# The second slab of six feed-forward networks, computed from 512-column products of high and low activations

## The chip, the cores and the metric

The kernel runs on one core of a Trainium2 chip. The metric is the device time in microseconds (us) of one execution, the median of several. The kernel before takes 1621.5 us (three runs, 1621.46 to 1623.59).

## What is computed

The reference runs a sequence of 256 tokens, 1024 wide, in float32 through four mixers (HGRN2, sparse attention, stick-breaking attention with a convolution, gated linear attention) and six feed-forward networks. Networks 0 and 1 have a causal convolution of width 3 on the up-projection; networks 2 to 5 have none. With `D_FF` = 2816:

```python
def conv_ffn(x, w_up, conv_w, conv_b, w_down):          # networks 0 and 1
    h = x @ w_up
    C = h.shape[-1]
    h = lax.conv_general_dilated(h, conv_w[:, None, :].astype(h.dtype), window_strides=(1,),
                                 padding=[(CONV_WIDTH - 1, 0)],
                                 dimension_numbers=('NWC', 'WIO', 'NWC'),
                                 feature_group_count=C) + conv_b
    gate, up = jnp.split(h, 2, axis=-1)
    return (jax.nn.silu(gate) * up) @ w_down

def swiglu(x, w_in, w_out):                              # networks 2 to 5
    a, b = jnp.split(x @ w_in, 2, axis=-1)
    return (jax.nn.silu(a) * b) @ w_out
```

## The kernel before

**Numbers in two parts.** Every weight and every activation is held as a high part and a low part (the value less its high part), and a product is high times high, plus high times low, plus low times high. ScalarE makes the high part of a slab of weights (`high`, line 596), VectorE the low part (`low`, line 1361, or `low_one`, line 1283).

**Slabs.** A feed-forward network has NF = 11 slabs of 256 hidden columns, numbered from 0. Slab i needs three pieces of weights of 1 MB each: its gate columns (ring slot `c_`), its up columns (slot `d`) and its rows of the down-projection (slot `a`). SyncE loads them in a fixed order, each when its slot is free. Slab 0 alone is computed with the tokens as rows and turned afterwards (`turn_tokens`); slab 10 has code of its own.

**TensorE's order in a network** is written out by hand in `ffn`: the products of slab 0, `up_one` (gate and up of slab 1), `down(0, True)`, `up_sums(2, True)`, `down(1)`, then a loop of `up_sums(j + 3)` and `down(j + 2)`, and the last slab. Into `up_one` the four transposes of `turn_tokens(1)` are put, which end slab 0. So the gate and up of a slab are computed one step ahead of its down-projection.

**Two forms of gate and up.** `up_one` (slab 1) uses `features`: for each of 4 blocks of 128 hidden columns and each of 8 chunks of the contraction it makes three 256-column matmuls (`three`, lines 1935 to 1937). The gate lies in half a bank of PSUM and the up in the other half, banks 6 and 7. `up_sums` (slabs 2 to 9, in networks 2 to 5 also slab 10) uses `high_sums` (line 2111: one 512-column matmul for each chunk, the high weights against high and low activations side by side) and `low_sums` (line 2118: one 256-column matmul for each chunk). There a bank holds two halves that must still be added: VectorE does it in `sum_parts` (line 1388), one for each of the 4 blocks, gate in banks 4 and 5, up in banks 6 and 7.

**The down-projection** `down` makes 24 matmuls of 512 columns: 12 for the first token block (`tb` = 0, banks 0 and 1), then 12 for the second (`tb` = 1, banks 2 and 3). It waits for the low part of `a` and for the gated activations (`g_hi` by ScalarE at line 784, `g_lo` by VectorE at line 1374).

**VectorE's and ScalarE's orders** are written by hand too, and each engine goes through its own strictly. After slab 0 (`body(0, ...)`, with lines 1447, 1368 and 1374) VectorE does, for a slab in the form of sums, `body_of_sums`:

```python
sum_parts(i, 0, 0)
sum_parts(i, 0, 1)
low(c_, i + c0)
if conv:
    later_taps(i, 0, range(2))
sum_parts(i, 1, 0)
sum_parts(i, 1, 1)
```

and then the taps of the up, the gating, the low parts of `d`, of the gated values and of `a`. ScalarE's `body_of_sums` does `gates(i)` (the first taps at line 757 in networks 0 and 1, the Silu at line 766 in the others), then `high(c_)`, `ups(i)`, `high(d)`, the two `split` (line 784) and `high(a)`. The `low(c_)` and `high(c_)` of slab i are for the weights of slab i + 1.

Of the kernel before, what the change touches and what calls it, by code (L numbers as in the profile page):

```python
# [26 lines left out]
P = 128  # L27
# [40 lines left out]
CROSS_BANK = {HG_HEADS: 4, GLA_HEADS: 5}  # L68
WIDE = 2 * SLAB
HALF_K = NK // 2  # L70
HGRN_PAIRS = ((0, 1), (2, 3), (0, 1), (2, 3))
# [69 lines left out]
def build(nc, A, out):  # L141
    with ExitStack() as ctx:
# [223 lines left out]
        def sums_before(f):  # L366
            return f * (NF - 2) - min(f, 2)

# [216 lines left out]
        def _(act):  # L585
# [124 lines left out]
            def ffn(conv, f_conv, f):  # L710

                a, b_, c_, d = FFN_SLOTS[f]
                q0, h0, s0, t0 = f * NF, f * (NF - 1), sums_before(f), f_conv * (NF - 3)

# [18 lines left out]

                def start_gate(b, i, odd):
                    up_done(b, i)
                    i = 0 if i is None else i
                    bank = ps[:, 4 + 2 * odd + b, :]
                    if conv:
                        for g in range(2):
                            c = i * 2 + (row_of["ffn_conv_w"] + f_conv * 132 + 88 + g * 22 + b)  # L740
                            cb = i * 2 + (row_of["ffn_conv_b"] + f_conv * 44 + g * 22 + b)
                            ins = act.activation(ff_c[:, b, g, :], bank[:, g * SEQ:g * SEQ + SEQ], ACT.Identity,
                                                 bias=cols[:, bass.ds(cb, 1)], scale=cols[:, bass.ds(c, 1)])
                        ins.then_inc(conv_in[b], 1)
                    else:
                        act.activation(ff_s[:, b, :], bank[:, 0:SEQ], ACT.Silu).then_inc(silu_done[b], 1)

                def conv_silu(b, nth):
                    act.wait_ge(conv_done[b], nth + (f_conv * 3 + 1))
                    act.activation(ff_s[:, b, :], ff_c[:, b, 0, :], ACT.Silu).then_inc(silu_done[b], 1)  # L750
# [17 lines left out]
                def ups(i):  # L768
                    if conv:
                        for b in range(2):  # L770
                            act.wait_ge(taps_done[0][b], i + (t0 - 1))
                            act.activation(ff_s[:, b, :], ff_c[:, b, 0, :], ACT.Silu).then_inc(silu_done[b], 1)
                        first_taps(1, i)
# [11 lines left out]

                def body(i, odd):
                    high(c_, i + c0, i * 16 + (mc + 16))
                    start_gate(0, i, odd)
                    start_gate(1, i, odd)
                    if conv:  # L790
                        conv_silu(0, i)
                    high(d, i + d0, i * 16 + (md + 16))
                    if conv:
                        conv_silu(1, i)
                    split(0, i, False)
                    split(1, i, False)
                    high(a, i + a0, i * 16 + (ma + 16))

                def alone(i, last=False):
                    for b in range(2):  # L800
                        start_gate(b, i if last else None, 0)
                    if conv:
                        conv_silu(0, 2 if last else i)
                        conv_silu(1, 2 if last else i)
                    split(0, i, last)
                    split(1, i, last)
# [11 lines left out]
                alone(0)  # L818
                body(1, 1)
                with act.Fori(0, NF - 3) as j:  # L820
# [316 lines left out]
        def _(dve):  # L1137
# [214 lines left out]
            def ffn(conv, f_conv, f):  # L1352
                a, b_, c_, d = FFN_SLOTS[f]
                q0, s0, t0 = f * NF, sums_before(f), f_conv * (NF - 3)
                low_one(c_)
# [20 lines left out]

                def sum_parts(i, g, b):

                    if g == 0 and b == 0:
                        dve.wait_ge(gate_half, i + (s0 - 1))  # L1380
                    elif g == 0:
                        dve.wait_ge(slab_used[c_], i + (used[c_] + 1))
                    elif b == 0:
                        dve.wait_ge(up_half, i + f * (NF - 1))
                    else:
                        dve.wait_ge(slab_used[d], i + (used[d] + 1))
                    halves_of = ps[:, 4 + 2 * g + b, :].rearrange("p (x t) -> p t x", x=2)
                    dve.tensor_reduce(ff_u[:, b, g, :], halves_of, AX_X, ALU.add).then_inc(part_sum[g][b], 1)  # L1388

                def later_taps(i, g, blocks):  # L1390

                    def tap(b, k):
                        shift = 2 - k
                        c = i * 2 + (row_of["ffn_conv_w"] + f_conv * 132 + k * 44 + g * 22 + b)
                        dst = ff_c[:, b, g, shift:SEQ]
                        return dve.scalar_tensor_tensor(dst, ff_u[:, b, g, 0:SEQ - shift], cols[:, bass.ds(c, 1)], dst,
                                                        ALU.mult, ALU.add)
                    for b in blocks:
                        dve.wait_ge(first_tap[g][b], i + (t0 - 1))
                        tap(b, 1).then_inc(mid_tap[g][b], 1)  # L1400
                    for b in blocks:
                        dve.wait_ge(mid_tap[g][b], i + (t0 - 1))
                        tap(b, 0).then_inc(taps_done[g][b], 1)

                def up_of(i, b):
                    if conv:
                        dve.wait_ge(taps_done[1][b], i + (t0 - 1))
                    else:
                        dve.wait_ge(part_sum[1][b], i + s0)
                    return ff_c[:, b, 1, :] if conv else ff_u[:, b, 1, :]  # L1410

                def body_of_sums(i):
                    sum_parts(i, 0, 0)
                    sum_parts(i, 0, 1)
                    low(c_, i + c0)
                    if conv:
                        later_taps(i, 0, range(2))
                    sum_parts(i, 1, 0)
                    sum_parts(i, 1, 1)
                    if conv:  # L1420
# [14 lines left out]

                def body(i, odd, nth, alone=False):
                    if not alone:
                        low(c_, i + c0)
                    if conv:
                        for b in range(2):  # L1440
                            bank = ps[:, 4 + 2 * odd + b, :]

                            def tap(g, k):
# [4 lines left out]
                                                                cols[:, bass.ds(c, 1)], dst, ALU.mult, ALU.add)  # L1448
                            dve.wait_ge(conv_in[b], nth + (f_conv * 3 + 1))
                            tap(0, 1).then_inc(tap_done[b], 1)  # L1450
                            tap(1, 1).then_inc(tap_done[b], 1)
                            dve.wait_ge(tap_done[b], nth * 2 + (f_conv * 6 + 2))
                            tap(0, 0)
                            tap(1, 0).then_inc(conv_done[b], 1)
                    for b in range(2):
                        gated(i, b, ff_c[:, b, 1, :] if conv else ps[:, 4 + 2 * odd + b, SEQ:2 * SEQ])
                    if not alone:
                        low(d, i + d0)
                    low_of_gated(i, nth == 2)
                    if not alone:  # L1460
                        low(a, i + (a0 + 1))

                low_one(a)
                body(0, 0, 0, True)
                body(1, 1, 1)
                with dve.Fori(0, NF - 3) as j:
# [5 lines left out]
                if conv:  # L1472
                    body(NF - 1, 0, 2, True)
                else:
# [454 lines left out]
        def _(pe):  # L1929
# [150 lines left out]
            def ffn(f, late=False, before_end=lambda: None):  # L2080

                a, b_, c_, d = FFN_SLOTS[f]
                q0, s0, conv = f * NF, sums_before(f), f < 2
                x0, x1 = x_new(), x_new()

# [9 lines left out]
                def up_one(after_first):  # L2095

                    pe.wait_ge(slab_ready[c_], used[c_] + 2)
                    for b in range(2):
                        ins = features(c_, 6 + b, b * P, P, 0)
                        if b == 0:  # L2100
                            after_first()
                    ins.then_inc(slab_used[c_], 1)
                    pe.wait_ge(slab_ready[d], used[d] + 2)
                    features(d, 6, 0, P, SEQ).then_inc(up_half, 1)
                    features(d, 7, P, P, SEQ).then_inc(slab_used[d], 1)

# [26 lines left out]
                def up_sums(i, second=False):  # L2133

                    for g, s in enumerate((c_, d)):
                        pe.wait_ge(slab_ready[s], i + (used[s] + 1))
                        for b in range(2):

                            if second:
                                pe.wait_ge(gt_done[b], q0 + 2 + g)  # L2140
                            else:
# [12 lines left out]
                def down(i, first=False):  # L2154
                    pe.wait_ge(slab_ready[a], i + (used[a] + 3))
                    pe.wait_ge(g_ready, i * 2 + (2 * q0 + 2))
                    for tb in range(NTB):
                        for b in range(2):
                            for half in range(2):
# [462 lines left out]
```

## Time and profile before

| | |
|---|---|
| median of three runs | 1621.5 us (1621.46 to 1623.59) |
| span of the profiled execution | 1619.9 us; the median is 1.6 us above it, and no other time of that execution is shown |
| TensorE (PE) busy | 1589.2 us, 98% of the span |
| VectorE (DVE) busy | 1172.7 us, 72% |
| ScalarE (ACT) busy | 856.8 us, 53% |
| GpSimd (POOL) busy | 79.1 us, 5% |

A matmul's record is longer than its share of TensorE's time, since successive matmuls overlap. How long a run of them takes is read from the start of the first to the start of what follows. A line of the timeline gives start, length, engine, line of the kernel, operation, output and inputs, shapes and count; in brackets stands the idle time before it and what ended it.

### The profile page before, as it was taken

The page shows a single profiled execution, that of the slowest core. Times are in us where ns is not written, and L with a number is a line of the kernel's source. Part 1 is how long each engine was busy: PE and PEld are TensorE (multiplying, and loading weights), DVE is VectorE, ACT ScalarE, POOL GpSimd, SP SyncE. Part 2 cuts the span into 40 slices and gives each one's busy share as a digit, 9 for nine tenths or more (in the row PEclk, how much of TensorE's full clock was granted, in tenths as well). Part 3 has the DMA queues.
Part 4 walks back from the last instruction along what each step waited for, and adds up shares of the span by engine and source line. Part 5 has one row for each costly group of instructions (what it writes and reads, how often), then busy time and mean ns, then how long its engine had stood idle before and what let it go on. Part 6 is the DMA issues. An engine that isn't in the chain of part 4 may idle for free. (4 is left out here: it accounts for less than half of the span.)

```text
span 1619.9 us, 25854 instructions
## 1 busy us (share of the span) xinstructions
PE 1589.2 (98%) x9921; PEld 1376.1 (85%) x9921; DVE 1172.7 (72%) x1771; ACT 856.8 (53%) x1198; POOL 79.1 (5%) x28
## 2 busy tenths in 40 slices
PE   8999999999999999999999999999999999999998
PEld 7978888889888887888889788888988888788887
DVE  5896787888577878666669766667666676776665
ACT  6334655565565556544466664447444474464443
POOL 0000000003400000000017300000000000000000
PEclk9999999999999999999999999999999999999999
DMA  9533567763345554555645445554656653445562
GB/s 296 188 110 127 180 186 218 208 171 129 118 138 200 181 196 168 194 183 195 218 160 166 128 145 187 202 202 148 208 183 206 203 202 116 146 143 182 190 199 78
DMA packets 211039, 283.40 MB, mean 175 GB/s; under 512 B 13196, under 2 KB 179075, under 8 KB 210963
## 3 DMA queue, kind: packets, MB, share of 16 engines
q1 hardware_dynamic: 209475, 278.18, 52.3%
q10 hardware_dynamic: 1488, 4.17, 0.8%
q8 instruction: 53, 0.87, 0.2%
q14 instruction: 23, 0.19, 0.0%
HBM read 280.88 MB, written 1.44 MB: 174 GB/s over the span
## 5 line engine op out<-in xcount | busy, mean ns | idle before, releaser
L596 ACT ACTIVATE w_hi<-raw 128x2048 fp32r<-128x2048 f32 x256 | 486.8, 1909 | 159.3 <-PE ps L2118 87.4
L1361 DVE TENSOR_TENSOR w_lo<-raw,w_hi 128x2048 fp32r<-128x2048 f32 x162 | 371.2, 2291 | 192.5 <-ACT w_hi L596 192.5
L2111 PE MATMUL ps<-x_pair,w_hi 128*128 128x512 f32 x1664 | 395.5, 390 | 0.0
L2111 PEld LDWEIGHTS ps<-x_pair,w_hi 128*128 128x128 f32 x1664 | 309.1, 188 | 62.0
L2118 PEld LDWEIGHTS ps<-x_pair,w_lo 128*128 128x128 f32 x1664 | 213.3, 191 | 8.1
L2118 PE MATMUL ps<-x_pair,w_lo 128*128 128x256 f32 x1664 | 215.8, 283 | 0.0
L1283 DVE TENSOR_TENSOR w_lo<-raw,w_hi 128x2048 fp32r<-128x2048 f32 x80 | 182.2, 2287 | 42.1 <-ACT w_hi L596 42.0
L1935 PE MATMUL ps<-x_pair,w_hi 128*128 128x256 f32 x688 | 196.1, 285 | 2.8 <-DVE x_pair L1191 1.4
L1937 PE MATMUL ps<-x_pair,w_lo 128*128 128x256 f32 x688 | 194.6, 283 | 0.0
L1936 PE MATMUL ps<-x_pair,w_hi 128*128 128x256 f32 x688 | 194.6, 283 | 0.0
L1935 PE MATMUL ps<-w_hi,g_hi 128*128 128x512 f32 x480 | 187.5, 391 | 0.0
L1936 PE MATMUL ps<-w_lo,g_hi 128*128 128x512 f32 x480 | 187.5, 391 | 0.0
L1937 PE MATMUL ps<-w_hi,g_lo 128*128 128x512 f32 x480 | 186.7, 389 | 0.0
L1935 PE MATMUL ps<-w_hi,x_pair 128*128 128x512 f32 (+1 forms) x432 | 174.0, 403 | 3.1 <-DVE x_pair L1191 2.9
L1937 PE MATMUL ps<-w_hi,x_pair 128*128 128x512 f32 (+1 forms) x432 | 167.3, 387 | 0.0
L1936 PE MATMUL ps<-w_lo,x_pair 128*128 128x512 f32 (+1 forms) x432 | 166.9, 386 | 0.0
L1388 DVE TENSOR_REDUCE arena<-ps 128x256 f32<-128x512 f32 x208 | 136.7, 684 | 9.0 <-PE ps L2118 7.4
L1935 PEld LDWEIGHTS ps<-x_pair,w_hi 128*128 128x128 f32 x688 | 131.1, 191 | 6.5 <-DVE w_lo L1283 3.3
L1936 PEld LDWEIGHTS ps<-x_pair,w_hi 128*128 128x128 f32 x688 | 131.2, 191 | 0.6
L1937 PEld LDWEIGHTS ps<-x_pair,w_lo 128*128 128x128 f32 x688 | 131.1, 191 | 0.2
L784 ACT ACTIVATE g_hi<-arena 128x256 fp32r<-128x256 f32 x120 | 44.1, 411 | 135.1 <-PE ps L1937 127.8
L1937 PEld LDWEIGHTS ps<-w_hi,g_lo 128*128 128x128 f32 x480 | 90.1, 188 | 19.2
(189 smaller groups left out, 1672.0 us busy)
## 6 DMA issues: line engine op xcount, KB each, us to landing
raw<-in_ffn_w_in SPq DMA_DIRECT2D x80, 1024.0 KB, 5.1
raw<-in_ffn_w_out SPq DMA_DIRECT2D x44, 1024.0 KB, 5.0
raw<-in_ffn_w_up SPq DMA_DIRECT2D x40, 1024.0 KB, 5.0
raw<-in_ffn_w_down SPq DMA_DIRECT2D x22, 1024.0 KB, 5.5
raw<-in_hgrn_w_in SPq DMA_DIRECT2D x16, 1024.0 KB, 7.9
raw<-in_gla_w_in SPq DMA_DIRECT2D x12, 1024.0 KB, 5.2
raw<-in_hyb_w_in SPq DMA_DIRECT2D x10, 1024.0 KB, 6.0
raw<-in_ffn_w_in SPq DMA_DIRECT2D x16, 512.0 KB, 4.5
```

Of the source, the lines that this page charges most:

```text
L596: act.activation(w_hi[slot][:, :], raw[slot][:, :], ACT.Copy).then_inc(hi_done[slot], 1)
L784: act.activation(dst[:, b, :], ff_g[:, b, :], ACT.Copy).then_inc(gt_hi[b], 1)
L1283: dve.tensor_tensor(w_lo[slot][:, :], raw[slot][:, :], w_hi[slot][:, :].bitcast(F32), ALU.subtract)\
L1361: dve.tensor_tensor(w_lo[slot][:, :], raw[slot][:, :], w_hi[slot][:, :].bitcast(F32), ALU.subtract)\
L1388: dve.tensor_reduce(ff_u[:, b, g, :], halves_of, AX_X, ALU.add).then_inc(part_sum[g][b], 1)
L1935: pe.matmul(out_ap, a_hi, b_hi, start=start, stop=False, skip_group_check=True)
L1936: pe.matmul(out_ap, a_hi, b_lo, start=False, stop=False, skip_group_check=True)
L1937: return pe.matmul(out_ap, a_lo, b_hi, start=False, stop=stop, skip_group_check=True)
L2111: pe.matmul(ps[:, bank, :], w_hi[s][:, at:at + P], x_pair[:, k, :, :].rearrange("p x t -> p (x t)"), start=k == 0, stop=False, skip_group_ ...
L2118: ins = pe.matmul(ps[:, bank, 0:SEQ], w_lo[s][:, at:at + P], x_hi[:, k, :], start=False, stop=k == NK - 1, skip_group_check=True)
```

## The change

Slab 1 of each network is computed in the form of the later slabs.

- TensorE: `up_one` makes for the gate (slot `c_`) and then the up (slot `d`) two `high_sums` and two `low_sums`. The gate goes to banks 6 and 7, the up to banks 2 and 3 (`sums_bank`). `turn_tokens(1)` comes after the first `high_sums`.
- TensorE: banks 2 and 3 are also those of the second token block in `down(0, True)`, so it waits ahead of `tb` = 1 until VectorE has added the halves of slab 1's up. In `up_sums(2, True)` the wait ahead of banks 6 and 7 is for the sums of slab 1's gate, where it was for its gating.
- VectorE and ScalarE: `body` for slab 1 is replaced by `body_of_sums`, in their order and with their operations. In networks 0 and 1 the taps read the sums in SBUF instead of PSUM.
- Counts that semaphores are compared with are shifted to match. No DMA is added, removed or moved.

```diff
+        def sums_bank(g, b, second=False):
+
+            return (6, 2)[g] + b if second else 4 + 2 * g + b
...
 (ScalarE)
-                def body(i, odd):
-                    high(c_, i + c0, i * 16 + (mc + 16))
-                    start_gate(0, i, odd)
-                    start_gate(1, i, odd)
-                    if conv:
-                        conv_silu(0, i)
-                    high(d, i + d0, i * 16 + (md + 16))
-                    if conv:
-                        conv_silu(1, i)
-                    split(0, i, False)
-                    split(1, i, False)
-                    high(a, i + a0, i * 16 + (ma + 16))
...
                 alone(0)
-                body(1, 1)
+                body_of_sums(SECOND)
...
 (VectorE)
-                    halves_of = ps[:, 4 + 2 * g + b, :].rearrange("p (x t) -> p t x", x=2)
+                    halves_of = ps[:, sums_bank(g, b, second), :].rearrange("p (x t) -> p t x", x=2)
...
-                body(0, 0, 0, True)
-                body(1, 1, 1)
+                body(0, 0)
+                body_of_sums(SECOND, True)
...
 (TensorE)
-                    pe.wait_ge(slab_ready[c_], used[c_] + 2)
-                    for b in range(2):
-                        ins = features(c_, 6 + b, b * P, P, 0)
-                        if b == 0:
-                            after_first()
-                    ins.then_inc(slab_used[c_], 1)
-                    pe.wait_ge(slab_ready[d], used[d] + 2)
-                    features(d, 6, 0, P, SEQ).then_inc(up_half, 1)
-                    features(d, 7, P, P, SEQ).then_inc(slab_used[d], 1)
+                    for g, s in enumerate((c_, d)):
+                        pe.wait_ge(slab_ready[s], used[s] + 2)
+                        for b in range(2):
+                            high_sums(s, sums_bank(g, b, True), b * P)
+                            if g == 0 and b == 0:
+                                after_first()
+                        for b in range(2):
+                            ins = low_sums(s, sums_bank(g, b, True), b * P)
+                            ins.then_inc(((gate_half, slab_used[c_]), (up_half, slab_used[d]))[g][b], 1)
...
-                            if second:
-                                pe.wait_ge(gt_done[b], q0 + 2 + g)
+                            if second and g == 0:
+                                pe.wait_ge(gt_done[b], q0 + 2)
+                            elif second:
+                                pe.wait_ge(part_sum[0][b], i + (s0 - 1))
...
                     for tb in range(NTB):
+                        if first and tb == 1:
+                            for b in range(2):
+                                pe.wait_ge(part_sum[1][b], s0 + SECOND)
```

## Rows read from the trace of the kernel before

**Rows 1.** The page: busy time of the engines, and busy tenths in 40 slices.
```profile
PE 1589.2 (98%) x9921; PEld 1376.1 (85%) x9921; DVE 1172.7 (72%) x1771; ACT 856.8 (53%) x1198; POOL 79.1 (5%) x28
...
PE   8999999999999999999999999999999999999998
```

**Rows 2.** TensorE's waits: total us, times, longest.
```profile
PE ps L2037 <- DVE xn L1216: 8.0, 8, 2.2
```

**Rows 3.** Timeline of TensorE, network 3, from up_one to down(1).
```profile
948.48 0.28 PE L1935 MATMUL ps<-x_pair,w_hi 128*128 128x256 f32 x1
...
951.35 0.60 PE L2091 MATMUL ps<-const,arena 128*128 128x128 f32 x4
951.71 0.36 PE L1935 MATMUL ps<-x_pair,w_hi 128*128 128x256 f32 x1
...
960.41 0.40 PE L1935 MATMUL ps<-w_hi,g_hi 128*128 128x512 f32 x1
...
965.88 3.79 PE L2111 MATMUL ps<-x_pair,w_hi 128*128 128x512 f32 x16
969.51 2.08 PE L2118 MATMUL ps<-x_pair,w_lo 128*128 128x256 f32 x16
971.42 3.82 PE L2111 MATMUL ps<-x_pair,w_hi 128*128 128x512 f32 x16
...
976.99 0.40 PE L1935 MATMUL ps<-w_hi,g_hi 128*128 128x512 f32 x1
```

**Rows 4.** Timeline of TensorE, network 0: start of up_one.
```profile
169.32 0.28 PE L1935 MATMUL ps<-x_pair,w_hi 128*128 128x256 f32 x1
```

**Rows 5.** Timeline of VectorE, network 0: slab 0, then sums of slab 2.
```profile
174.16 3.46 DVE L1447 SCALAR_TENSOR_TENSOR arena<-ps,cols,arena 128x255 f32<-128x255 f32 x8
...
178.45 0.99 DVE L1374 TENSOR_TENSOR g_lo<-arena,g_hi 128x256 fp32r<-128x256 f32 x2
...
192.82 1.28 DVE L1388 TENSOR_REDUCE arena<-ps 128x256 f32<-128x512 f32 x2
196.72 2.29 DVE L1361 TENSOR_TENSOR w_lo<-raw,w_hi 128x2048 fp32r<-128x2048 f32 x1 [2.62 <-ACT w_hi L596]
198.93 1.66 DVE L1396 SCALAR_TENSOR_TENSOR arena<-arena,cols 128x255 f32<-128x255 f32 x4
200.50 1.28 DVE L1388 TENSOR_REDUCE arena<-ps 128x256 f32<-128x512 f32 x2
...
204.57 2.29 DVE L1361 TENSOR_TENSOR w_lo<-raw,w_hi 128x2048 fp32r<-128x2048 f32 x1
```

**Rows 6.** Timeline of ScalarE, network 0: first taps and high(c_) of slab 2.
```profile
193.76 1.12 ACT L757 ACTIVATE arena<-arena,cols 128x256 f32<-128x256 f32 x2 [3.67 <-DVE arena L1388]
194.79 1.90 ACT L596 ACTIVATE w_hi<-raw 128x2048 fp32r<-128x2048 f32 x1
```

**Rows 7.** Timeline of VectorE, network 3: slab 0, then sums of slab 2.
```profile
954.22 0.76 DVE L1374 TENSOR_TENSOR g_lo<-arena,g_hi 128x256 fp32r<-128x256 f32 x2 [0.15 <-ACT g_hi L784]
...
970.92 1.40 DVE L1388 TENSOR_REDUCE arena<-ps 128x256 f32<-128x512 f32 x2
...
976.81 1.28 DVE L1388 TENSOR_REDUCE arena<-ps 128x256 f32<-128x512 f32 x2
```

**Rows 8.** Timeline of TensorE: the same turn and products ahead of networks 2 and 3.
```profile
637.83 1.97 PE L2037 MATMUL ps<-const,xn 128*128 128x128 f32 x8 [2.17 <-DVE xn L1216]
...
641.10 0.40 PE L1935 MATMUL ps<-w_hi,x_pair 128*128 128x512 f32 x1
...
940.91 1.06 PE L2037 MATMUL ps<-const,xn 128*128 128x128 f32 x8
...
942.51 0.41 PE L1935 MATMUL ps<-w_hi,x_pair 128*128 128x512 f32 x1
```

**Rows 9.** Stretches: us, engines' busy time, granted clock, DMA share, GB/s.
```profile
341.00:345.00 4.00, 2.63 (x18) 2.37 (x18) 2.88 (x9) 2.72 (x12) 0.00 (x0) 1.00 0.36 126
...
638.00:640.00 2.00, 2.00 (x9) 1.72 (x10) 1.55 (x5) 1.44 (x6) 0.00 (x0) 0.50 0.00 0
```

More of the change, by code:

```diff
@@ L69 @@
 WIDE = 2 * SLAB
+SECOND = 1
 HALF_K = NK // 2
@@ L366, in sums_before @@
         def sums_before(f):
-            return f * (NF - 2) - min(f, 2)
+            return f * (NF - 1) - min(f, 2)
+        def sums_bank(g, b, second=False):
+            return (6, 2)[g] + b if second else 4 + 2 * g + b
         def halves(t, m):
@@ L712, in ffn @@
                 a, b_, c_, d = FFN_SLOTS[f]
-                q0, h0, s0, t0 = f * NF, f * (NF - 1), sums_before(f), f_conv * (NF - 3)
+                q0, h0, s0, t0 = f * NF, f * (NF - 1), sums_before(f) + 1, f_conv * (NF - 2)
                 act.wait_ge(tok_done, f + 1)
@@ L732, in up_done, with start_gate @@
                         act.wait_ge(slab_used[d], i + (d0 + 1))
-                def start_gate(b, i, odd):
+                def start_gate(b, i):
                     up_done(b, i)
                     i = 0 if i is None else i
-                    bank = ps[:, 4 + 2 * odd + b, :]
+                    bank = ps[:, 4 + b, :]
                     if conv:
@@ L748, in conv_silu @@
                 def conv_silu(b, nth):
-                    act.wait_ge(conv_done[b], nth + (f_conv * 3 + 1))
+                    act.wait_ge(conv_done[b], nth + (f_conv * 2 + 1))
                     act.activation(ff_s[:, b, :], ff_c[:, b, 0, :], ACT.Silu).then_inc(silu_done[b], 1)
@@ L770, in ups @@
                         for b in range(2):
-                            act.wait_ge(taps_done[0][b], i + (t0 - 1))
+                            act.wait_ge(taps_done[0][b], i + t0)
                             act.activation(ff_s[:, b, :], ff_c[:, b, 0, :], ACT.Silu).then_inc(silu_done[b], 1)
@@ L784, in split @@
                     act.activation(dst[:, b, :], ff_g[:, b, :], ACT.Copy).then_inc(gt_hi[b], 1)
-                def body(i, odd):
-                    high(c_, i + c0, i * 16 + (mc + 16))
-                    start_gate(0, i, odd)
-                    start_gate(1, i, odd)
-                    if conv:
-                        conv_silu(0, i)
-                    high(d, i + d0, i * 16 + (md + 16))
-                    if conv:
-                        conv_silu(1, i)
-                    split(0, i, False)
-                    split(1, i, False)
-                    high(a, i + a0, i * 16 + (ma + 16))
                 def alone(i, last=False):
                     for b in range(2):
-                        start_gate(b, i if last else None, 0)
+                        start_gate(b, i if last else None)
                     if conv:
-                        conv_silu(0, 2 if last else i)
-                        conv_silu(1, 2 if last else i)
+                        conv_silu(0, 1 if last else i)
+                        conv_silu(1, 1 if last else i)
                     split(0, i, last)
@@ L1353, in ffn @@
                 a, b_, c_, d = FFN_SLOTS[f]
-                q0, s0, t0 = f * NF, sums_before(f), f_conv * (NF - 3)
+                q0, s0, t0 = f * NF, sums_before(f) + 1, f_conv * (NF - 2)
                 low_one(c_)
@@ L1375, in low_of_gated, with sum_parts @@
                             .then_inc(g_ready, 1)
-                def sum_parts(i, g, b):
+                def sum_parts(i, g, b, second=False):
                     if g == 0 and b == 0:
@@ L1398, in later_taps @@
                     for b in blocks:
-                        dve.wait_ge(first_tap[g][b], i + (t0 - 1))
+                        dve.wait_ge(first_tap[g][b], i + t0)
                         tap(b, 1).then_inc(mid_tap[g][b], 1)
                     for b in blocks:
-                        dve.wait_ge(mid_tap[g][b], i + (t0 - 1))
+                        dve.wait_ge(mid_tap[g][b], i + t0)
                         tap(b, 0).then_inc(taps_done[g][b], 1)
@@ L1406, in up_of @@
                     if conv:
-                        dve.wait_ge(taps_done[1][b], i + (t0 - 1))
+                        dve.wait_ge(taps_done[1][b], i + t0)
                     else:
@@ L1410, in up_of, with body_of_sums @@
                     return ff_c[:, b, 1, :] if conv else ff_u[:, b, 1, :]
-                def body_of_sums(i):
-                    sum_parts(i, 0, 0)
-                    sum_parts(i, 0, 1)
+                def body_of_sums(i, second=False):
+                    sum_parts(i, 0, 0, second)
+                    sum_parts(i, 0, 1, second)
                     low(c_, i + c0)
@@ L1417, in body_of_sums @@
                         later_taps(i, 0, range(2))
-                    sum_parts(i, 1, 0)
-                    sum_parts(i, 1, 1)
+                    sum_parts(i, 1, 0, second)
+                    sum_parts(i, 1, 1, second)
                     if conv:
@@ L1434, in last_body, with body @@
                     low_of_gated(i, True)
-                def body(i, odd, nth, alone=False):
-                    if not alone:
-                        low(c_, i + c0)
+                def body(i, nth):
                     if conv:
                         for b in range(2):
-                            bank = ps[:, 4 + 2 * odd + b, :]
+                            bank = ps[:, 4 + b, :]
                             def tap(g, k):
@@ L1448, in tap @@
                                                                 cols[:, bass.ds(c, 1)], dst, ALU.mult, ALU.add)
-                            dve.wait_ge(conv_in[b], nth + (f_conv * 3 + 1))
+                            dve.wait_ge(conv_in[b], nth + (f_conv * 2 + 1))
                             tap(0, 1).then_inc(tap_done[b], 1)
                             tap(1, 1).then_inc(tap_done[b], 1)
-                            dve.wait_ge(tap_done[b], nth * 2 + (f_conv * 6 + 2))
+                            dve.wait_ge(tap_done[b], nth * 2 + (f_conv * 4 + 2))
                             tap(0, 0)
@@ L1455, in body @@
                     for b in range(2):
[L1456 to L1461, printed above, removed]
+                        gated(i, b, ff_c[:, b, 1, :] if conv else ps[:, 4 + b, SEQ:2 * SEQ])
+                    low_of_gated(i, nth == 1)
                 low_one(a)
-                body(0, 0, 0, True)
-                body(1, 1, 1)
+                body(0, 0)
+                body_of_sums(SECOND, True)
                 with dve.Fori(0, NF - 3) as j:
@@ L1472, in ffn @@
                 if conv:
-                    body(NF - 1, 0, 2, True)
+                    body(NF - 1, 1)
                 else:
@@ L2082, in ffn @@
                 a, b_, c_, d = FFN_SLOTS[f]
-                q0, s0, conv = f * NF, sums_before(f), f < 2
+                q0, s0, conv = f * NF, sums_before(f) + 1, f < 2
                 x0, x1 = x_new(), x_new()
```

## The prediction

> **What bounds the kernel now.** I read the page first: TensorE is busy in 98% of the span and in every slice [rows 1]. Then its waits: the longest group, eight waits for VectorE, comes to 8.0 us of 1619.9, the longest single one being 2.2 us [rows 2], and none lies between `up_one` and the end of a network. So the time is TensorE's work in its own order, and the change can act in two ways only: fewer microseconds of matmuls, or a new wait. I then read the timelines of TensorE, VectorE and ScalarE around slab 1 of a network with convolution and of one without [rows 3 to 7], and last what a wait of TensorE does to its clock [rows 8, 9]. A difference of about 0.2% (3.2 us) is what can be told from no change here.
>
> **TensorE's work.** In network 3 `up_one` runs from 948.48 to 960.41: 11.93 us, of which the four transposes take 951.71 − 951.35 = 0.36 [rows 3]; so 96 matmuls of 256 columns take 11.57 us, 120.5 ns each. The form it is given stands in the same rows: `up_sums` of slab 2 runs from 965.88 to 976.99, 11.11 us for 32 matmuls of 512 columns (3.63 us for 16, 227 ns each) and 32 of 256 (1.91 us for 16, 119 ns each) [rows 3]. The transposes stay at 0.36. `up_one` will take 11.47 us, 0.46 less, six times: **−2.8 us**. The columns streamed are equal, 24576; the gain is some 13 ns for each of 32 matmuls that disappear.
>
> The Trainium skill (TensorE: Matmul & The Clock Gate, section "Back-to-back issue gap") gives for isolated matmuls a spacing of N / 2.4 + 2.5 ns, so only 2.5 ns for each matmul that disappears: 0.08 us a network, an estimate from that page. The trace shows 227 ns where that formula gives 216, so the rows stay in the sum.
>
> **VectorE's chain behind slab 1.** No work is costly in itself: four sums, 1.28 us for two [rows 5], are added a network to an engine busy 72%, and ScalarE keeps the same number of operations. What matters is order. `down(0, True)` now waits ahead of `tb` = 1 for the sums of the up, and in VectorE's order `low(c_)` stands ahead of these; in networks 0 and 1 the gate's later taps do as well. `low(c_)` needs `high(c_)`, which now stands behind `gates(1)` on ScalarE, and those need VectorE's first sums. Before, nothing on TensorE waited for this chain so early.
>
> Its length is that of slab 2 in network 0, where nothing in it waits for TensorE: the first sums start at 192.82; ScalarE's two first taps start at 193.76, its `high(c_)` at 194.79 and takes 1.90 [rows 6]; `low(c_)` starts at 196.72; taps at 198.93; the up's sums at 200.50, and they end at 201.78 [rows 5]. From first to last: 8.96 us.
>
> When does it start? VectorE must first finish slab 0, ending with `g_lo` at 178.45 + 0.99 = 179.44 [rows 5]. `turn_tokens(1)` comes 24 × 0.1195 − 8 × 0.227 = 1.05 us earlier in the new `up_one`, but this does not help: the taps of slab 0 start at 174.16 [rows 5] without idle time, straight after `low_one(a)`, whose own inputs the change leaves alone. Successive operations overlap by 0.08 (198.93 against 196.72 + 2.29) [rows 5], so the chain starts at 179.36. The gate itself will be there: `up_one` starts at 169.32 [rows 4], and the gate's last matmul is issued by 169.32 + 0.36 + 5.56 = 175.24. The chain ends at 179.36 + 8.96 = 188.32.
>
> TensorE will reach `down(0, True)` at 169.32 + 11.47 = 180.79 and, after half of the 5.47 us of `down` [rows 3], `tb` = 1 at 183.53. It stands for 188.32 + 0.06 (estimated way of a semaphore) − 183.53 = **4.85 us**. I add 0.1 for the restart: a first matmul after other work is up to 0.1 us longer than its fellows, as 0.36 against 0.28 [rows 3]. Network 1 has the same distances to within 0.03 us. Two networks: 2 × 4.95 = **+9.9 us**.
>
> **The clock.** Ahead of network 2 TensorE stood for 2.17 us; then eight transposes and three matmuls took 641.10 − 637.83 = 3.27 us, where ahead of network 3 the same took 942.51 − 940.91 = 1.60 [rows 8]. In the first case the granted clock was 0.50, that is 1.2 GHz in place of 2.4; where the page had a wait of 1.43 us (in the stretch 341 to 345) it stayed at 1.00 [rows 9]. That fall cost 1.67 us. A stand of 4.85 us, over twice the one that brought a fall, will bring one, part of which may lie inside the stand. Bounds: nothing, and two such prices (3.3 us), a network. I take 1.5, nearest to the one row: **+3.0 us**. All other engines run on meanwhile, so it is TensorE alone that pays.
>
> **Networks without convolution.** In network 3 `g_lo` ends at 954.98 [rows 7], so the sums start at 954.90. There the chain has no later taps: 970.92 to 976.81 + 1.28 = 978.09 is 7.17 us, of which 0.12 waits for TensorE (1.40 for two sums against 1.28) [rows 7]. It ends at 954.90 + 7.05 = 961.95. TensorE wants `tb` = 1 at 948.48 + 11.47 + 2.74 = 962.69. No stand, with 0.7 us to spare; networks 4 and 5 have the same distances, network 2 has 0.6 us more. Should the cover go, each microsecond of delay costs one, in four networks.
>
> **What is late next.** In network 0 with the chain started at S = 179.36, `low(c_)` ends at S + 6.19 = 185.6, ahead of `up_sums(2)` at 191.2. `low(d)` starts at S + 11.75 [rows 5] and ends at 193.4; it is wanted at 196.7. Behind it stand `g_lo` and `low(a)` (0.75 and 2.29), ending at about 196.4, wanted by `down(1)` at 202.3. The next sums find their gate ready at 195.8, as before. SyncE's loads start when these low parts are done, one step ahead of use: `c_` of slab 3 is issued at 185.6 and wanted by ScalarE only behind sums that start at 196.4. So nothing follows; the stand is paid once a network. Neither SP's nor POOL's queue gets or loses an instruction in the networks.
>
> **Sum.** −2.8 + 9.9 + 3.0 = +10.1 us. The span of 1619.9 becomes 1630.0; the median stands 1.6 above the span, so 1631.6 us.
>
> **The rivals.**
> - *The clock stays up*, or the fall lies inside the stand. For: other waits, up to 1.43 us, brought none. Against: the fall after 2.17 us. Time: 1621.5 − 2.8 + 9.9 = 1628.6. Chance 0.18.
> - *No stand* (the other side): the chain in networks 0 and 1 ends by 183.5, so it would have to be 4.85 us shorter, for instance if `high(c_)` and `low(c_)` did not lie in it. Then only the matmuls count: 1621.5 − 2.8 = 1618.7, within 0.2%. Against: both stand ahead of the up's sums in code that each engine goes through strictly. A chain that is shortened by 3 us or more gives a result within 0.2% as well. Chance 0.05.
> - *The cover of 0.7 us goes* in networks 2 to 5, by slower sums or a later `high(c_)`: with 1 us of stand in each, +4, 1635.6. Chance 0.08.
> - *The matmuls give nothing*, the pitch being one of columns alone. TensorE would come 0.46 later and stand 4.4 us: 1621.5 + 2 × 4.5 + 3.0 = 1633.5 us. Against it are the two pitches of rows 3. The page's rule comes near to this (by its formula 0.5 us gained in all, an estimated 1633.2). Chance 0.04.
>
> **Numbers.** The forecast has 0.65. Its own range is 1629 to 1634, by the clock's price. With the rival without a fall below and a double fall (3.3 us a network, 1635.2) above, and 1 us for the chain's length at the lower end, I give 1627.5 to 1635.5. Slower by over 0.2% is every case but the missing stand: 0.94; within 0.2%: 0.05; faster by over 0.2% would need more than the matmuls can give: 0.01.
>
> **What the changed profile would show.** TensorE waiting for VectorE's sums (line 1388 before, a few lines off after) twice, some 4.9 us each, inside `down(0)` of networks 0 and 1, and not in the other four; `up_one` at 11.47 us; a granted clock of 0.50 behind each wait; on VectorE sums, `low(c_)`, taps, sums in this order with 8.96 us from end to end. The prediction fails if the chain starts earlier than `g_lo` of slab 0, if the wait shows in all six networks, or if loads come late in the loops that follow.

## The result, and the profile after

The changed kernel takes 1633.88 us (median of five runs, 1633.45 to 1634.47) against 1621.5 us before: a ratio of 1.0074, 95% interval 1.0063 to 1.0085. It is slower by 12.4 us, where +10.1 us was forecast. The profiled span grew by 12.2 us, from 1619.9 to 1632.1.

From the page of the changed kernel, to be read against [rows 1]:

```profile
span 1632.1 us, 25506 instructions
...
PE 1591.2 (97%) x9729; PEld 1368.6 (84%) x9729; DVE 1187.1 (73%) x1795; ACT 858.0 (53%) x1198; POOL 79.0 (5%) x28
```

TensorE has 192 matmuls fewer, 32 in each network, and still counts as busy for 2 us longer: some of its matmuls ran at the lower clock. Its waits (us in total, times, longest), against [rows 2]:

```profile
PE ps L1921 <- DVE arena L1380: 9.0, 2, 4.5
PE ps L2023 <- DVE xn L1208: 8.1, 7, 2.2
```

The first line is new: twice TensorE waits for VectorE's sums. The timeline of TensorE in network 0 has the place:

```profile
170.09 1.98 PE L2097 MATMUL ps<-x_pair,w_hi 128*128 128x512 f32 x8
171.91 0.60 PE L2077 MATMUL ps<-const,arena 128*128 128x128 f32 x4
172.26 2.10 PE L2097 MATMUL ps<-x_pair,w_hi 128*128 128x512 f32 x8
174.20 2.07 PE L2104 MATMUL ps<-x_pair,w_lo 128*128 128x256 f32 x16
176.11 3.82 PE L2097 MATMUL ps<-x_pair,w_hi 128*128 128x512 f32 x16
...
184.20 0.39 PE L1923 MATMUL ps<-w_hi,g_lo 128*128 128x512 f32 x1
189.11 0.76 PE L1921 MATMUL ps<-w_hi,g_hi 128*128 128x512 f32 x1 [4.52 <-DVE arena L1380]
189.67 0.63 PE L1922 MATMUL ps<-w_lo,g_hi 128*128 128x512 f32 x1
...
193.93 1.32 PE L2097 MATMUL ps<-x_pair,w_hi 128*128 128x512 f32 x5
```

`up_one` starts at 170.09 and `tb` = 1 could start 0.23 us behind 184.20, at 184.43. It starts at 189.11: a stand of 4.68 us. Its 12 matmuls then take 193.93 − 189.11 = 4.82 us, where half a `down` took 2.73 before: 2.1 us for the clock. VectorE's timeline of the same stretch holds the chain, against [rows 5]:

```profile
179.79 0.43 DVE L1366 TENSOR_TENSOR g_lo<-arena,g_hi 128x256 fp32r<-128x256 f32 x1 [0.15 <-ACT g_hi L789]
180.13 1.28 DVE L1380 TENSOR_REDUCE arena<-ps 128x256 f32<-128x512 f32 x2
183.89 2.29 DVE L1353 TENSOR_TENSOR w_lo<-raw,w_hi 128x2048 fp32r<-128x2048 f32 x1 [2.47 <-ACT w_hi L601]
186.10 1.66 DVE L1388 SCALAR_TENSOR_TENSOR arena<-arena,cols 128x255 f32<-128x255 f32 x4
187.68 1.28 DVE L1380 TENSOR_REDUCE arena<-ps 128x256 f32<-128x512 f32 x2
```

Sums, 2.47 us of idle time for ScalarE's high part, `low(c_)`, taps, sums: 180.13 to 188.96, 8.83 us. The stretches of 2 us around the restart (busy PE, PEld, DVE, ACT and POOL, then the granted clock):

```profile
184.00:186.00 2.00, 0.58 (x3) 0.16 (x1) 2.00 (x1) 0.00 (x0) 0.00 (x0) 1.00 0.00 0
186.00:188.00 2.00, 0.00 (x0) 0.00 (x0) 2.00 (x6) 0.60 (x2) 0.00 (x0) 0.64 0.22 48
188.00:190.00 2.00, 0.89 (x2) 0.83 (x3) 1.81 (x4) 1.81 (x4) 0.00 (x0) 0.50 1.04 353
190.00:192.00 2.00, 2.00 (x6) 1.52 (x6) 2.00 (x6) 1.40 (x1) 0.00 (x0) 0.50 0.35 123
192.00:194.00 2.00, 2.00 (x8) 1.57 (x7) 1.77 (x1) 0.00 (x0) 0.00 (x0) 0.65 0.00 0
194.00:196.00 2.00, 2.00 (x11) 1.62 (x9) 0.76 (x2) 1.81 (x3) 0.00 (x0) 1.00 0.51 145
```

The clock fell from 2.4 to 1.2 GHz (0.50) while TensorE stood, and came back near the end of the 12 matmuls. Network 3 has no wait; there `up_one` and `down(0)` take 978.85 − 961.80 = 17.05 us, against 17.40 in [rows 3]:

```profile
961.80 1.98 PE L2097 MATMUL ps<-x_pair,w_hi 128*128 128x512 f32 x8
...
978.85 1.52 PE L2097 MATMUL ps<-x_pair,w_hi 128*128 128x512 f32 x6
```

From the start of `up_one` to that of `up_sums(2)`, network by network: 17.41, 17.42, 17.50, 17.40, 17.41, 17.41 us before; 23.84, 24.09, 17.18, 17.05, 17.06, 17.05 after. That is +13.1 in two networks and −1.4 in four, +11.7 us of the 12.2. The rest lies elsewhere: TensorE's first work came 0.9 us later for a DMA that is in both kernels (`up_one` of network 0 starts 0.8 us later), and the stretch ahead of network 2, where the clock did not fall this time, is 0.2 us shorter.

### The profile page after: what moved, and what is told of

Read it like the earlier page. It is cut to its first block and busy times, and to the rows that moved or that the text cites. A ratio compares the mean times of both kernels' runs of the same rounds, so it can differ in the third digit from the quotient of the medians.

```text
span 1632.1 us, 25506 instructions
## 1 busy us (share of the span) xinstructions
PE 1591.2 (97%) x9729; PEld 1368.6 (84%) x9729; DVE 1187.1 (73%) x1795; ACT 858.0 (53%) x1198; POOL 79.0 (5%) x28
## 5 line engine op out<-in xcount | busy, mean ns | idle before, releaser
L2097 PE MATMUL ps<-x_pair,w_hi 128*128 128x512 f32 x1856 | 443.0, 390 | 1.0 <-DVE w_lo L1275 1.0
L2097 PEld LDWEIGHTS ps<-x_pair,w_hi 128*128 128x128 f32 x1856 | 344.2, 188 | 70.4 <-DVE w_lo L1275 1.5
L2104 PEld LDWEIGHTS ps<-x_pair,w_lo 128*128 128x128 f32 x1856 | 238.0, 191 | 9.1
L2104 PE MATMUL ps<-x_pair,w_lo 128*128 128x256 f32 x1856 | 240.7, 283 | 0.0
L1380 DVE TENSOR_REDUCE arena<-ps 128x256 f32<-128x512 f32 x232 | 152.3, 684 | 9.1 <-PE ps L2104 7.4
L1921 PE MATMUL ps<-x_pair,w_hi 128*128 128x256 f32 (+1 forms) x496 | 141.4, 285 | 1.4 <-DVE x_pair L1183 1.4
L1922 PE MATMUL ps<-x_pair,w_hi 128*128 128x256 f32 (+1 forms) x496 | 140.3, 283 | 0.0
L1923 PE MATMUL ps<-x_pair,w_lo 128*128 128x256 f32 (+1 forms) x496 | 140.3, 283 | 0.0
L1921 PEld LDWEIGHTS ps<-w_hi,g_hi 128*128 128x128 f32 x480 | 91.4, 190 | 27.3 <-DVE arena L1380 9.8
L1922 PEld LDWEIGHTS ps<-w_lo,g_hi 128*128 128x128 f32 x480 | 91.5, 191 | 16.7
L1921 PEld LDWEIGHTS ps<-w_hi,x_pair 128*128 128x128 f32 x432 | 81.2, 188 | 24.3 <-issue 5.8
```

Source lines behind the costliest of these rows:

```text
L1921: pe.matmul(out_ap, a_hi, b_hi, start=start, stop=False, skip_group_check=True)
L1922: pe.matmul(out_ap, a_hi, b_lo, start=False, stop=False, skip_group_check=True)
L1923: return pe.matmul(out_ap, a_lo, b_hi, start=False, stop=stop, skip_group_check=True)
L2097: pe.matmul(ps[:, bank, :], w_hi[s][:, at:at + P], x_pair[:, k, :, :].rearrange("p x t -> p (x t)"), start=k == 0, stop=False, skip_group_ ...
L2104: ins = pe.matmul(ps[:, bank, 0:SEQ], w_lo[s][:, at:at + P], x_hi[:, k, :], start=False, stop=k == NK - 1, skip_group_check=True)
```

## The experiments

A loss of 12 us in two waits leaves two questions. Is it the order of the work behind slab 1, as the prediction has it, or the use of banks 2 and 3 and the added sums? And what would be left of the change with the wait gone? All times are medians beside the kernel before on the same chip (1621.68 us with the first four, 1621.93 with the last three).

### The up's sums first

```diff
                 def body_of_sums(i, second=False):
                     sum_parts(i, 0, 0, second)
                     sum_parts(i, 0, 1, second)
+                    if second:
+                        sum_parts(i, 1, 0, second)
+                        sum_parts(i, 1, 1, second)
                     low(c_, i + c0)
...
-                    sum_parts(i, 1, 0, second)
-                    sum_parts(i, 1, 1, second)
+                    if not second:
+                        sum_parts(i, 1, 0, second)
+                        sum_parts(i, 1, 1, second)
```

> Slab 1 alone: VectorE adds all four sums of gate and up before low(c_) and the gate's taps. If the loss is the chain of low(c_) and taps ahead of the up's sums, no stand is left in down(0) of networks 0 and 1 (the up's last sum should end some 12.7 us after the start of up_one, and tb = 1 is reached at 14.3), the clock stays at 1.00 there, low(c_) ends some 16 us after the start of up_one and is wanted at 17.1, and what is left is the matmuls' gain of 0.35 us a network: 1621.5 - 2.1 = 1619.4. If the loss came from more work on VectorE or from the use of banks 2 and 3 in itself, the time stays near 1634.

Measured: 1624.77 us (1624.4 to 1625.16), ratio 1.0019, interval 1.0010 to 1.0028. The stand in `down(0)` is gone in both networks and 9.1 us of the loss with it, so these 9.1 us were a matter of order: banks 2 and 3 and the added sums are still there. But 3.1 us over before stay, where 2.1 below it were expected. Networks 2 to 5 have their 17.05 us (17.18 in network 2). Networks 0 and 1 reach `up_sums(2)` at 17.05 us too, and then lose 2.6 to 2.7 us each up to the start of the next `up_one`. The first bit is seen on TensorE:

```profile
186.18 3.79 PE L2101 MATMUL ps<-x_pair,w_hi 128*128 128x512 f32 x16
189.80 2.07 PE L2108 MATMUL ps<-x_pair,w_lo 128*128 128x256 f32 x16
192.47 3.92 PE L2101 MATMUL ps<-x_pair,w_hi 128*128 128x512 f32 x16 [0.59 <-DVE w_lo L1353]
...
209.30 3.92 PE L2101 MATMUL ps<-x_pair,w_hi 128*128 128x512 f32 x16
```

The up of slab 2 starts at 192.47, that of slab 3 at 209.30: 16.83 us, and so on to the last slab, where a step took 16.57 before. The reason stands in VectorE's timeline:

```profile
179.17 2.48 DVE L1380 TENSOR_REDUCE arena<-ps 128x256 f32<-128x512 f32 x4
...
193.00 2.28 DVE L1353 TENSOR_TENSOR w_lo<-raw,w_hi 128x2048 fp32r<-128x2048 f32 x1
195.21 1.28 DVE L1380 TENSOR_REDUCE arena<-ps 128x256 f32<-128x512 f32 x2
199.11 2.29 DVE L1353 TENSOR_TENSOR w_lo<-raw,w_hi 128x2048 fp32r<-128x2048 f32 x1 [2.62 <-ACT w_hi L601]
...
212.03 1.28 DVE L1380 TENSOR_REDUCE arena<-ps 128x256 f32<-128x512 f32 x2
...
312.97 1.28 DVE L1380 TENSOR_REDUCE arena<-ps 128x256 f32<-128x512 f32 x2
```

From the sums of slab 2 to those of slab 9 it is (312.97 − 195.21) / 7 = 16.82 us a slab, with no wait for TensorE. VectorE had the very same pace before: [rows 5] have the sums of slab 2 at 192.82, and those of slab 9 stand at 310.59, so 16.82 too:

```profile
310.59 1.28 DVE L1388 TENSOR_REDUCE arena<-ps 128x256 f32<-128x512 f32 x2
```

So in networks 0 and 1 VectorE's round (the time from one slab's sums to the next slab's) is 0.25 us longer than TensorE's. Before, this was covered by what VectorE had in hand when the loop began, and these seven steps used up 1.75 us of it. This is what the prediction had not seen.

How much VectorE had in hand can be read from the distance between the start of a slab's gate on TensorE and its sums on VectorE. It is 8.42 us in this run once TensorE is held up (212.03 − 203.61, where TensorE's gate of slab 3 starts at 203.61), and it was 192.82 − 186.73 = 6.09 us at slab 2 before: 2.3 us in hand. In this run slab 2 starts at 195.21 − 186.18 = 9.03 us, with nothing in hand. Of the 2.9 us between the two, 0.35 is TensorE being earlier. The rest is that VectorE needs 195.21 − 179.17 = 16.04 us from the end of slab 0 to the sums of slab 2, where it took 192.82 − 179.36 = 13.46 us before (179.36 as in the prediction); the four added sums take 2.48 us in a row. So it is the added sums, above all, that use up what VectorE had in hand; this is worked out from the rows, and no run took the sums out alone. The loss adds up: the up of slab 2 comes 192.47 − 186.18 − 5.54 = 0.75 us late, and seven steps of 0.25 follow, 2.5 of the 2.6 to 2.7 us.

### The taps behind the up's sums

```diff
                     low(c_, i + c0)
-                    if conv:
+                    if conv and not second:
                         later_taps(i, 0, range(2))
                     sum_parts(i, 1, 0, second)
                     sum_parts(i, 1, 1, second)
+                    if conv and second:
+                        later_taps(i, 0, range(2))
```

> Slab 1 alone, networks 0 and 1: the gate's later taps go behind the up's sums, low(c_) stays ahead of them. If the stand is the sum of the chain's links, it shrinks by the taps' 1.58 us, from 4.7 to 3.1 in each of the two networks: 1633.9 - 3.2 = 1630.7, and down to 1628.5 if the fall of the clock gets cheaper with the shorter stand. If TensorE waited for something outside that chain: 1633.9.

Measured: 1629.15 us (1626.95 to 1629.58), ratio 1.0047, interval 1.0032 to 1.0063, 4.7 us below the changed kernel. The stand in its trace is 2.95 us in network 0 and 2.94 in network 1 (idle time), 1.57 and 1.59 less than 4.52 and 4.53: the link taken out is 1.58 us long. In this execution the clock did not fall behind the two stands. It is the shortest of the four (1626.95 us); the others took 1.9 to 2.6 us more, and whether the clock fell in them no trace shows. The last three steps of network 0, from one `down` to the next, took 16.67, 16.81 and 16.87 us, those ahead of them 16.57: VectorE's start in hand, which the first experiment shows to matter, was used up near the end.

### ScalarE's high part first

```diff
                 def body_of_sums(i, second=False):
+                    if conv and second:
+                        high(c_, i + c0, i * 16 + (mc + 16))
                     gates(i)
-                    high(c_, i + c0, i * 16 + (mc + 16))
+                    if not (conv and second):
+                        high(c_, i + c0, i * 16 + (mc + 16))
```

> Slab 1 alone, networks 0 and 1: ScalarE makes high(c_) ahead of the gate's first taps. If the detour over ScalarE is a link of the chain, VectorE's idle time ahead of low(c_) (2.5 us) shrinks to about 0.3, and the stand from 4.7 to 2.5: 1633.9 - 4.4 = 1629.5, or 1627 with a cheaper fall of the clock. If the loss were VectorE's own work alone, ScalarE's order would change nothing: 1633.9.

Measured: 1627.02 us (1624.13 to 1628.12), ratio 1.0031, interval 1.0020 to 1.0041. VectorE's idle time ahead of `low(c_)` is 0.18 us, the stands are 2.22 and 2.23:

```profile
179.46 1.28 DVE L1383 TENSOR_REDUCE arena<-ps 128x256 f32<-128x512 f32 x2
180.92 2.29 DVE L1356 TENSOR_TENSOR w_lo<-raw,w_hi 128x2048 fp32r<-128x2048 f32 x1 [0.18 <-ACT w_hi L601]
```

In this one execution the clock fell in network 1 and not in network 0, with equal stands. From `up_one` to `up_sums(2)` it is 21.14 us with the fall and 19.52 without: 1.6 us. Runs with a fall in both networks and runs with none would lie 3.2 us apart; the shortest and the longest here lie 4 us apart. Only one of them has a trace, so that this is the cause is not shown.

### The stand filled with matmuls

```diff
                         if first and tb == 1:
+                            if conv:
+                                keep_warm(21, 4)
                             for b in range(2):
```

> The changed kernel with 21 matmuls of 512 columns of zeros (bf16, into bank 4, which nobody needs then) ahead of the wait in down(0) of networks 0 and 1, some 4.6 us in which TensorE stood. The stand is thus filled and its length kept. If the fall of the clock costs 2.1 and 2.35 us, as the 12 matmuls behind the stand show, the clock stays at 1.00 and the time is 1633.9 - 4.4 = 1629.5. If the price of the clock were only the 1.5 us a network that was predicted: 1630.9; if none: 1633.9.

Measured: 1629.59 us (1628.8 to 1630.2), ratio 1.0049, interval 1.0034 to 1.0064. That is 4.3 us less than the changed kernel. The stand is now work, as long as before (188.58 − 183.90 = 4.68 us), and the 12 matmuls behind it take 191.42 − 188.58 = 2.84 us where they took 4.82. From `up_one` to `up_sums(2)` it is 21.86 us in both networks, 1.98 and 2.23 less than in the changed kernel: 4.2 of the 4.3 us is the clock's.

```profile
183.90 4.71 PE L2015 MATMUL ps<-const 128*128 128x512 bf16 x21
188.58 0.47 PE L1921 MATMUL ps<-w_hi,g_hi 128*128 128x512 f32 x1
...
191.42 0.84 PE L2097 MATMUL ps<-x_pair,w_hi 128*128 128x512 f32 x3
```

### Both orders together

The first experiment left a loop of 16.82 us, in which VectorE is idle for 2.62 us ahead of `low(c_)`. So ScalarE's order was changed in all slabs of networks 0 and 1, on top of the first experiment.

```diff
                 def body_of_sums(i):
+                    if conv:
+                        high(c_, i + c0, i * 16 + (mc + 16))
                     gates(i)
-                    high(c_, i + c0, i * 16 + (mc + 16))
+                    if not conv:
+                        high(c_, i + c0, i * 16 + (mc + 16))
```

> The kernel with all four sums of slab 1 first, and in every body of sums of networks 0 and 1 ScalarE makes high(c_) ahead of the gate's first taps. If what was left of the loss is VectorE's and ScalarE's loop of 16.82 us a slab against TensorE's 16.57, into which high(c_) puts 2.6 us of idle time on VectorE, that loop now follows TensorE at 16.57, TensorE waits nowhere in networks 0 and 1, and all six networks gain 0.35 us: 1621.7 - 2.1 = 1619.6. If the 16.82 us came from VectorE's work or from TensorE's side, it stays near 1624.8.

Measured: 1619.61 us (1619.04 to 1620.01), ratio 0.9985, interval 0.9976 to 0.9994: 0.15% below before. VectorE's idle time ahead of `low(c_)` is gone at slab 2 and 1.2 to 1.3 us in the later slabs, where it was 2.62. What is left there is not the detour: ScalarE itself waits for TensorE ahead of `high(c_)`, and VectorE follows TensorE (the sums of slabs 4 to 9 start 16.57 or 16.58 us apart):

```profile
194.66 1.28 DVE L1383 TENSOR_REDUCE arena<-ps 128x256 f32<-128x512 f32 x2
195.86 2.29 DVE L1356 TENSOR_TENSOR w_lo<-raw,w_hi 128x2048 fp32r<-128x2048 f32 x1
...
225.14 1.46 DVE L1383 TENSOR_REDUCE arena<-ps 128x256 f32<-128x512 f32 x2
225.90 1.92 ACT L601 ACTIVATE w_hi<-raw 128x2048 fp32r<-128x2048 f32 x1 [3.01 <-PE ps L2111]
227.85 2.29 DVE L1356 TENSOR_TENSOR w_lo<-raw,w_hi 128x2048 fp32r<-128x2048 f32 x1 [1.26 <-ACT w_hi L601]
```

### ScalarE's order in the kernel before

The same edit of ScalarE's `body_of_sums` in the kernel before, and nothing else.

> The kernel before with the same order on ScalarE (high(c_) ahead of the gate's first taps in the bodies of sums of networks 0 and 1) and nothing else. There VectorE's loop of 16.82 us starts with enough in hand that TensorE keeps to 16.57, so nothing should change: 1621.7. If the order helps by itself, the time falls by some 2 us and the gain of the kernel with both edits isn't the form's.

Measured: 1621.86 us (1621.06 to 1622.96) beside 1621.93, ratio 0.9998, interval 0.9989 to 1.0007. VectorE's idle time ahead of `low(c_)` falls from 2.62 to 0.33 us at slab 2 and to 1.26 in the later slabs, its sums start 16.57 us apart from slab 3 on, and the time does not move. So the order by itself gives nothing; it is needed once slab 1 takes VectorE's start in hand away.

### Four networks only

Networks 2 to 5 as in the changed kernel, networks 0 and 1 as before. The two forms are chosen by `conv` at each place that the change touches, for instance:

```diff
-                body(1, 1)
+                if conv:
+                    body(1, 1)
+                else:
+                    body_of_sums(SECOND)
```

> Only networks 2 to 5 have slab 1 in the form of sums, networks 0 and 1 are as before. If these four have no wait, up_one and down(0) together take 17.05 in place of 17.40 us in each and the time is 1621.7 - 1.4 = 1620.3, within 0.2%. If the new form costs something there that the profile hides (as a fall of the clock), the time is above 1621.7.

Measured: 1620.6 us (1620.1 to 1621.57), ratio 0.9991, interval 0.9982 to 1.0000. The size is that of four times 0.35 us; the interval ends at no change.

## Why the prediction was right, and where not

**The stand** was right in place, kind and number: inside `down(0)` of networks 0 and 1, for the sums of the up, in no other network. Its size was 4.68 us against 4.85. The chain started where it was put, 10.04 us behind `up_one` (180.13 − 170.09, and 179.36 − 169.32 in the prediction), and was 8.83 us long against 8.96; TensorE came 0.12 us later than forecast. The 0.06 us for the way of a semaphore stood on no row; from the end of the sums to TensorE's start it was 189.11 − 188.96 = 0.15. Taking links out (taps 1.58 us, the detour over ScalarE 2.3 us) shortened the stand by as much each time, and taking `low(c_)` and the taps out removed it.

**The matmuls' gain** was mis-sized: 0.35 us a network, not 0.46, so −2.1 and not −2.8. The sum had the pace inside long runs right, but left out a restart: the second eight `high_sums` take 174.20 − 172.26 = 1.94 us behind the transposes, the first eight 171.91 − 170.09 = 1.82. That `down(0)` is reached 11.59 us after `up_one`'s start, not 11.47, is this 0.12. The Trainium skill (TensorE: Matmul & The Clock Gate, section "Back-to-back issue gap") would give 0.08 us a network, an estimate from its 2.5 ns for each isolated matmul; the trace has over four times that, and does not agree.

**The clock** was right in kind, small in size: 3.0 us was taken for both networks, the traces show 2.1 and 2.35, and filling the stand gave 4.3 us back. (The 2.1 and 2.35 hold some 0.1 us each for the restart, which the prediction had counted with the stand.) It had been priced from the one fall seen before, behind a stand half as long; the bounds of nothing and 3.3 us a network held it.

**The sum** by these sizes is −2.1 + 2 × 4.68 + 4.4 = +11.7 us, with 10.1 forecast and 12.4 measured; the stretches from `up_one` to `up_sums(2)` give the same 11.7.

**What failed** is the rival of no stand. It said that only the matmuls' gain would count then, 1618.7 us; the kernel without stand took 1624.8. The step behind it was "What is late next": it followed the chain through one slab only and took the loops that follow as TensorE's. For the changed kernel this came out right, because the stand itself gave VectorE its start in hand (8.42 − (198.96 − 193.93) = 3.4 us at slab 2, by the rows of the changed kernel): TensorE's steps are 16.57 us. That VectorE's round in networks 0 and 1 is 16.82 us could have been read before, from the distance of two starts of the sums in a row. What tells that this was the cause, and not the new form, is that the reordered ScalarE changes nothing before (1621.86 beside 1621.93) and takes away 5.4 us in the kernel without the stand: from 3.1 us above its kernel before (1624.77 beside 1621.68) to 2.3 below (1619.61 beside 1621.93).

**The networks without convolution** kept their cover of 0.7 us: in network 3 the up's sums start at 974.00 and end at 975.28, and TensorE starts `tb` = 1 at 976.13, 0.85 us later, of which 0.15 would be the way to TensorE as in network 0. The gain measured there alone is in keeping with 0.35 us each.

## What to carry to other kernels

When work takes a form that another engine must finish, count how far down that engine's own fixed order the finishing step lies, from its earliest possible start: here the sums that TensorE wanted were the last 1.3 us of a chain of 8.8. Compare the rounds of the engines as well: here VectorE's round was 0.25 us longer than that of TensorE, which set the time, and TensorE never waited for it while VectorE had a start in hand. A change that takes that start away, if only by 2.5 us of added sums, makes the slower round set the time. And a wait of TensorE can cost more than its length: 4.7 us stood cost another 2.1 to 2.3 us at the lower clock.

## What the runs showed of the hardware

The length of a stand alone did not tell whether the clock falls. Behind stands of 2.9 us it stayed at 2.4 GHz in both networks of one execution; behind 2.22 and 2.23 us it fell in one network and stayed in the other. Behind 2.17 us ahead of network 2 it fell before [rows 8, 9] and stayed in the changed kernel, where the eight transposes took 1.09 us:

```profile
651.75 1.09 PE L2023 MATMUL ps<-const,xn 128*128 128x128 f32 x8 [2.17 <-DVE xn L1208]
```

All nine traces have this stand, of 2.14 to 2.18 us, and the clock fell in six of them. It need not fall inside the stand: it did so once, 0.2 us before the transposes, and in the others up to 2.2 us after TensorE had started again. Behind stands of 4.7 us it fell both times. What decides it stays open.

A fall of the clock also need not cost what the matmuls behind it lose. Ahead of network 2 they lost 1.67 us before, but TensorE waits for VectorE several times on the way to the next `up_one`, and these waits took up most of it. From the first eight transposes to the next eight it was 645.80 − 637.83 = 7.97 us before and 659.47 − 651.75 = 7.72 in the changed kernel; to the next `up_one` it is 16.53 or 16.54 us in the three traces without a fall and 16.56 to 16.91 in the six with one.
